# A buffer that nothing uses, ahead of the stage buffers of a two-layer trunk step

## The chip, the cores and the metric

The kernel runs on 1 core of a Trainium2 chip. The metric is device time in microseconds (us); the kernel before takes 2651.89 us, the median of 3 runs.

## What is computed

The reference is one inference step of a trunk with two layers (model width 2048), for 128 context tokens and 128 latent tokens. Layer 0 mixes tokens by differential attention beside grouped-query attention, layer 1 by a bidirectional mLSTM beside latent attention; each layer then has a gated FFN with a 3-tap convolution over tokens. Norms are RMS norms, and shift, scale and gate come from a conditioning vector through w_mod. Cut to what matters:

```python
for l in range(DEPTH):                               # DEPTH = 2
    mod = split(silu(cond) @ w_mod[l] + b_mod[l], 6)     # w_mod: 2048 x 12288
    h = rms(x, norm1_g[l]) * (1 + mod[1]) + mod[0]
    if l % 2 == 0:
        out = merge(diff_attention(...), gqa(...)) @ even_w_out   # from h @ even_w_in (2048 x 4608)
    else:
        out = merge(mlstm(...), mla(...)) @ odd_w_out             # from h @ odd_w_in (2048 x 4960)
    x = x + mod[2] * out
    h = rms(x, norm2_g[l]) * (1 + mod[4]) + mod[3]
    u = dwconv(h @ ffn_w_up[l], conv_w[l], conv_b[l])             # 2048 x 11264
    g, up = split(u, 2)
    x = x + mod[5] * ((silu(g) * up) @ ffn_w_down[l])             # 5632 x 2048
y = rms(x, final_norm_g)
```

The context tokens run as a second stream through the same weights, with a conditioning vector of their own. Everything is float32.

## The kernel before, in words

**Weights.** All large weights come as slabs of 512 KB (128 partitions x 2 chunks x 512 columns). `load_order` plans the order of all loads once, and SyncE issues them into 8 slots of `raw`. ScalarE rounds a slab to float32r in `w_hi` (`split_hi`, L491), VectorE subtracts to get the rest in `w_lo` (`split_lo`, L498); both hold 4 slabs. TensorE waits for `w_lo`, computes, and frees the slab.

**Products.** Tokens lie along the free dimension: both streams are 256 columns. An activation tile is split like a weight: in the stage's buffer `xs` (128 x 16 x 512, float32r) columns 0 to 255 of a chunk are the high part and 256 to 511 the low part. `three_products` (L633) computes one weight tile of 128 x 128 against 256 moving columns in three matmuls, each with a weight load of its own:

```python
pe.matmul(made, hi, x_hi, start=start and not second, ...)      # L636
pe.matmul(made, hi, x_lo, start=False, ...)                     # L637
return pe.matmul(made, lo, x_hi, start=False, stop=stop, ...)   # L638
```

In `pe.matmul(out, weights, moving)` the second operand is loaded into the array and the third streams past it. A slab is 2 chunks x 4 tiles x 3 products = 24 matmuls (`tile_products`, L640).

**Order.** Phases run one after another, and within a phase slabs in a fixed order (`Phase.seq`): modulation (`w_mod`), the even layer's input projection (72 slabs), its output projection, the FFN of layer 0 (up: 11 iterations x 2 groups x 8 slabs; down: 88 slabs), the odd layer's tail, q/k and v/o projections, latent query and key/value products, output projection, the FFN of layer 1. Modulation slabs (`mod_products`, L592) are spread over the phases up to the odd layer's v/o projection: after every 4 slabs of the phase come 4 modulation slabs, which break into the stream of the three products. The down projection of layer 0 and both parts of the FFN of layer 1 have none. Beside the products, ScalarE and VectorE do the splits, copies out of PSUM, convolution, attention and norms, placed by slab number.

**Places in SBUF.** A partition's buffers are laid out in the order in which `sb` (L319) is called. The persistent ones come first, in `trunk` at L326 to L343; the buffers of a stage are allocated inside a scope behind them and given back at its end, so that each stage starts at the same byte. In the built program of the kernel before the places per partition are, in bytes:

| buffer | starts at | past a multiple of 512 |
|---|---|---|
| raw, w_hi, w_lo, x (L326 to L329) | 16,512; 49,280; 65,664; 82,048 | 128 |
| m0, the last persistent one (L343) | 116,256 | 32 |
| first buffer of each stage: xs_even, acts, mix1 | 116,288 | 64 |
| xs_ffn of both layers (L1081) | 161,344 | 64 |
| xs_odd (L2210) | 179,264 | 64 |
| xs_out1b and xs_out1a, cq (L1905, L1906, L1900) | 182,336; 198,720; 182,336 | 64 |
| last end of any buffer (tb_out1) | 227,392 | |

A chunk of `xs` is 2048 bytes, its low part starts 1024 bytes behind its high part, and a full weight tile is 512 bytes wide. So all moving operands of the three products start 64 bytes past a multiple of 512, and all full weight tiles 128 past one. Two unused buffers are there already: `lead` (48 columns, L341) and `lead_odd` (24 columns, L2208), the second of which lies ahead of `xs_odd`. In the latent value products (`ukv_products`, L1957) the roles are changed: `w_hi` and `w_lo` move (256 columns in two pieces of 128), and the latent `ckv_hi` or `ckv_lo` is loaded.

Of the kernel before, what the change touches and what calls it, by code (L numbers as in the profile page):

```python
# [27 lines left out]
P = 128  # L28
# [287 lines left out]
def trunk(nc, ins, outs):  # L316
    ctx = ExitStack()
    with ctx:
        def sb(name, shape, dt=F32, scope=ctx):  # L319
            return scope.enter_context(nc.sbuf_tensor(name, shape, dt))  # L320
# [20 lines left out]
        lead = sb("lead", [P, LEAD_COLUMNS])  # L341
        gate_b = sb("gate_b", [4 * HEADS, 1])
        m0 = sb("m0", [2 * HEADS, 2])  # L343
        banks = ctx.enter_context(nc.psum_tensor("banks", [P, 8, 512], F32))

        ident = const[:, C_IDENT:C_IDENT + P]
# [2173 lines left out]
```

How the kernel before makes its waits and increments, by code:

```python
def wait(eng, sem, value):  # L177
    if not isinstance(value, int) or value > 0:
        eng.wait_ge(sem, value)
# [305 lines left out]
        def split_hi(act, f, i, o):  # L486
            q, s = f.own(i, o), f.own_at[o]
            act.wait_ge(*slab_landed(f, i, s))
            wait(act, slab_used.sem, q - SPLIT + 1)
            act.activation(w_hi[:, o % SPLIT], raw[:, s % RAW], ACT.Copy).then_inc(hi_done.sem, 1)
# [1 line left out]
        def split_lo(dve, f, i, o):  # L493
            q, s = f.own(i, o), f.own_at[o]
            dve.wait_ge(hi_done.sem, q + 1)
            wait(dve, slab_used.sem, q - SPLIT + 1)
            dve.tensor_tensor(w_lo[:, o % SPLIT], raw[:, s % RAW], w_hi[:, o % SPLIT].bitcast(F32),
                              ALU.subtract).then_inc(lo_done.sem, 1)
# [57 lines left out]
            def body(i, first, last):  # L557
                for s, (kind, g, k) in enumerate(f.seq):
                    if kind == "mod":
                        pe.wait_ge(*slab_landed(f, i, s))
                        mod_products(pe, f, i, s, g, k).then_inc(mod_used.sem, 1)
                    else:
                        o = f.own_at.index(s)
                        pe.wait_ge(lo_done.sem, f.own(i, o) + 1)
                        if k == 0:
                            out = 2 * (f.group(i, g) - 1)
# [28 lines left out]
        def copy_mod_rows(act, f, i, p):  # L596
            n = f.pair(i, p)
            act.wait_ge(mod_used.sem, f.mod_slab(i, MOD_SLABS * (PAIR * p + PAIR - 1) + MOD_SLABS - 1) + 1)
            wait(act, rows_turned.sem, n)
```

## Time and profile before

| what | us |
|---|---|
| median of 3 runs | 2651.89 |
| the 3 runs | 2647.7 to 2652.81 |
| the profiled execution's own time | 2675.88 |
| its span, from the first to the last instruction | 2674.1 |

The span is one profiled execution. PE is TensorE's matmuls, PEld its weight loads, DVE VectorE, ACT ScalarE, SP SyncE. A matmul's duration runs from its issue to its last result, and matmuls are pipelined: the step from one start to the next is much shorter than a duration. So the durations of a group add up to more than its share of the span, and the pace is read from counts in a stretch in which PE has no pause. A window's count holds every instruction of which a part lies in it.

### The profile page before, as it was taken

The page shows a single profiled execution, that of the slowest core. Times are in us where ns is not written, and L with a number is a line of the kernel's source. Part 1 is how long each engine was busy: PE and PEld are TensorE (multiplying, and loading weights), DVE is VectorE, ACT ScalarE, POOL GpSimd, SP SyncE. Part 2 cuts the span into 40 slices and gives each one's busy share as a digit, 9 for nine tenths or more (in the row PEclk, how much of TensorE's full clock was granted, in tenths as well). Part 3 has the DMA queues.
Part 4 walks back from the last instruction along what each step waited for, and adds up shares of the span by engine and source line. Part 5 has one row for each costly group of instructions (what it writes and reads, how often), then busy time and mean ns, then how long its engine had stood idle before and what let it go on. Part 6 is the DMA issues. An engine that isn't in the chain of part 4 may idle for free. (4 is left out here: it accounts for less than half of the span.)

```text
span 2674.1 us, 52531 instructions
## 1 busy us (share of the span) xinstructions
PE 2550.9 (95%) x20826; PEld 2328.3 (87%) x20826; DVE 1485.3 (56%) x1970; ACT 1295.8 (48%) x1795; POOL 11.7 (0%) x20
## 2 busy tenths in 40 slices
PE   6799999989999999999989999789899999999997
PEld 1487988878888888899989889778899999999997
DVE  1334455655454545577765445645655565567676
ACT  1443444364444444466565444334655555556553
POOL 0000000000000000000000000000000000000000
PEclk9999999989999999999989998889899999999999
DMA  9886665768888888865646884123455555555553
GB/s 388 330 317 233 231 228 184 289 256 309 318 316 319 314 318 313 321 212 192 203 128 234 321 299 142 62 93 114 156 189 186 184 187 185 185 188 187 176 186 107
DMA packets 170060, 608.28 MB, mean 227 GB/s; under 512 B 18688, under 2 KB 25152, under 8 KB 169648
## 3 DMA queue, kind: packets, MB, share of 16 engines
q1 hardware_dynamic: 168624, 600.33, 64.0%
q10 hardware_dynamic: 512, 2.97, 0.3%
q0 software_dynamic: 768, 2.79, 0.3%
q8 instruction: 112, 1.84, 0.3%
q14 instruction: 44, 0.36, 0.0%
HBM read 601.38 MB, written 4.63 MB: 227 GB/s over the span
## 5 line engine op out<-in xcount | busy, mean ns | idle before, releaser
L498 DVE TENSOR_TENSOR w_lo<-raw,w_hi 128x1024 fp32r<-128x1024 f32 x756 | 925.5, 1225 | 966.3 <-ACT w_hi L491 964.6
L491 ACT ACTIVATE w_hi<-raw 128x1024 fp32r<-128x1024 f32 x756 | 798.7, 1057 | 1018.2 <-PE banks L638 994.2
L636 PE MATMUL banks<-xs_ffn,w_hi 128*128 128x256 f32 x4224 | 1188.3, 281 | 5.2 <-DVE xs_ffn L792 5.0
L637 PE MATMUL banks<-xs_ffn,w_hi 128*128 128x256 f32 x4224 | 1181.9, 280 | 0.0
L638 PE MATMUL banks<-xs_ffn,w_lo 128*128 128x256 f32 x4224 | 1181.7, 280 | 0.0
L636 PEld LDWEIGHTS banks<-xs_ffn,w_hi 128*128 128x128 f32 x4224 | 797.8, 189 | 43.5 <-issue 42.6
L638 PEld LDWEIGHTS banks<-xs_ffn,w_lo 128*128 128x128 f32 x4224 | 803.8, 190 | 0.0
L637 PEld LDWEIGHTS banks<-xs_ffn,w_hi 128*128 128x128 f32 x4224 | 795.3, 188 | 0.0
L592 PE MATMUL banks<-raw,cond 128*32 128x512 f32 x1536 | 227.2, 609 | 29.2 <-DMA raw<-in_w_mod 18.0
L636 PE MATMUL banks<-xs_even,w_hi 128*128 128x256 f32 x832 | 241.8, 291 | 10.0 <-DVE w_lo L498 5.9
L637 PE MATMUL banks<-xs_even,w_hi 128*128 128x256 f32 x832 | 233.3, 280 | 0.0
L638 PE MATMUL banks<-xs_even,w_lo 128*128 128x256 f32 x832 | 233.2, 280 | 0.0
L636 PEld LDWEIGHTS banks<-xs_even,w_hi 128*128 128x128 f32 x832 | 158.8, 191 | 34.2 <-issue 22.9
L636 PE MATMUL banks<-xs_odd,w_hi 128*128 128x256 f32 (+2 forms) x640 | 181.3, 283 | 2.7 <-DVE xs_odd L792 2.6
L637 PE MATMUL banks<-xs_odd,w_hi 128*128 128x256 f32 (+2 forms) x640 | 179.0, 280 | 0.0
L638 PE MATMUL banks<-xs_odd,w_lo 128*128 128x256 f32 (+2 forms) x640 | 178.8, 279 | 0.0
L592 PEld LDWEIGHTS banks<-raw,cond 128*32 128x32 f32 x1536 | 43.5, 109 | 147.8 <-DMA raw<-in_w_mod 77.5
L637 PEld LDWEIGHTS banks<-xs_even,w_hi 128*128 128x128 f32 x832 | 158.4, 190 | 1.0 <-issue 1.0
L638 PEld LDWEIGHTS banks<-xs_even,w_lo 128*128 128x128 f32 x832 | 158.5, 190 | 0.0
L1071 DVE SCALAR_TENSOR_TENSOR y<-u,par,y 128x254 f32<-128x254 f32 x352 | 146.2, 478 | 20.5 <-ACT y L1058 17.6
L636 PEld LDWEIGHTS banks<-xs_odd,w_hi 128*128 128x128 f32 (+2 forms) x640 | 119.9, 187 | 14.0 <-issue 12.9
L1129 DVE TENSOR_TENSOR xs_ffn<-acts,xs_ffn 128x512 fp32r<-128x512 f32 x176 | 120.4, 684 | 0.0
(305 smaller groups left out, 2054.2 us busy)
## 6 DMA issues: line engine op xcount, KB each, us to landing
raw<-in_w_mod SPq DMA_DIRECT2D x384, 512.0 KB, 6.7
raw<-in_ffn_w_up SPq DMA_DIRECT2D x352, 512.0 KB, 3.5
raw<-in_ffn_w_down SPq DMA_DIRECT2D x176, 512.0 KB, 4.1
raw<-in_even_w_in SPq DMA_DIRECT2D x72, 512.0 KB, 4.0
raw<-in_odd_w_in SPq DMA_DIRECT2D x64, 512.0 KB, 4.5
raw<-in_even_w_out SPq DMA_DIRECT2D x32, 512.0 KB, 3.7
raw<-in_odd_w_out SPq DMA_DIRECT2D x32, 512.0 KB, 3.2
raw<-in_odd_w_tail SPq DMA_DIRECT2D x8, 448.0 KB, 3.7
```

Source lines behind the costliest of these rows:

```text
L491: act.activation(w_hi[:, o % SPLIT], raw[:, s % RAW], ACT.Copy).then_inc(hi_done.sem, 1)
L498: dve.tensor_tensor(w_lo[:, o % SPLIT], raw[:, s % RAW], w_hi[:, o % SPLIT].bitcast(F32), ALU.subtract).then_inc(lo_done.sem, 1)
L592: mm = pe.matmul(banks[quad:quad + QUAD, f.mod_bank(p), :], cond[:, n, columns], raw[:, s % RAW, c, :], start=n < QUADS and not second, st ...
L636: pe.matmul(made, hi, x_hi, start=start and not second, stop=False, skip_group_check=second)
L637: pe.matmul(made, hi, x_lo, start=False, stop=False, skip_group_check=second)
L638: return pe.matmul(made, lo, x_hi, start=False, stop=stop, skip_group_check=second)
L1071: added = dve.scalar_tensor_tensor(yt, ut, weight(f, i, g, which, t), yt, ALU.mult, ALU.add)
L1129: dve.tensor_tensor(xs[:, slot_of(s), NT:2 * NT], acts[:, chunk0(s):chunk0(s) + CHUNKS], xs[:, slot_of(s), 0:NT].bitcast(F32), ALU.subtrac ...
```

## The change

Behind `m0`, the last persistent buffer, a buffer of 112 columns of float32 is allocated, 448 bytes in each partition. Nothing reads or writes it. The whole diff:

```diff
@@ -341,6 +341,7 @@
         lead = sb("lead", [P, LEAD_COLUMNS])
         gate_b = sb("gate_b", [4 * HEADS, 1])
         m0 = sb("m0", [2 * HEADS, 2])
+        stage_pad = sb("stage_pad", [P, 112])
         banks = ctx.enter_context(nc.psum_tensor("banks", [P, 8, 512], F32))
```

So each stage's first buffer starts at 116,288 + 448 = 116,736 = 228 x 512, and all stage buffers that started 64 past a multiple of 512 start at one. The persistent buffers, `raw`, `w_hi`, `w_lo` and `x` among them, stay where they are.

## Rows read from the trace of the kernel before

**Rows 1.** The page: busy us, share of span, instructions; granted clock in tenths.

```profile
PE 2550.9 (95%) x20826; PEld 2328.3 (87%) x20826; DVE 1485.3 (56%) x1970; ACT 1295.8 (48%) x1795; POOL 11.7 (0%) x20
...
PEclk9999999989999999999989998889899999999999
```

**Rows 2.** Windows: length, busy (count) per engine, clock, DMA share, GB/s.

```profile
1160.00:1360.00 200.00, 200.00 (x1767) 200.00 (x1766) 144.77 (x170) 120.80 (x156) 0.00 (x0) 1.00 0.60 193
2000.00:2200.00 200.00, 200.00 (x1701) 200.00 (x1700) 119.12 (x148) 105.79 (x129) 0.00 (x0) 1.00 0.56 186
1920.00:2645.00 725.00, 724.82 (x6152) 724.30 (x6151) 460.48 (x559) 404.88 (x511) 0.00 (x0) 1.00 0.55 183
```

**Rows 3.** Groups by form, 1940 to 2640 us, PE: busy us, mean ns.

```profile
L636 PE MATMUL banks<-xs_ffn,w_hi 128*128 128x256 f32 x1982 | 556.9, 281 | 0.0
L638 PE MATMUL banks<-xs_ffn,w_lo 128*128 128x256 f32 x1982 | 556.9, 281 | 0.0
```

**Rows 4.** Groups by form, 1140 to 1370 us, PE.

```profile
L636 PE MATMUL banks<-xs_ffn,w_hi 128*128 128x256 f32 x676 | 186.7, 276 | 0.0
L637 PE MATMUL banks<-xs_ffn,w_hi 128*128 128x256 f32 x676 | 186.6, 276 | 0.0
L638 PE MATMUL banks<-xs_ffn,w_lo 128*128 128x256 f32 x675 | 186.3, 276 | 0.0
```

**Rows 5.** Groups by form, 1940 to 2640 us, weight loads.

```profile
L638 PEld LDWEIGHTS banks<-xs_ffn,w_lo 128*128 128x128 f32 x1982 | 380.5, 192 | 0.0
L636 PEld LDWEIGHTS banks<-xs_ffn,w_hi 128*128 128x128 f32 x1982 | 372.1, 188 | 0.0
```

**Rows 6.** Groups by form, 1140 to 1370 us, weight loads.

```profile
L638 PEld LDWEIGHTS banks<-xs_ffn,w_lo 128*128 128x128 f32 x676 | 126.9, 188 | 0.0
```

**Rows 7.** Windows between breaks of the first FFN's up projection.

```profile
620.00:630.00 10.00, 10.00 (x87) 10.00 (x86) 3.23 (x4) 3.45 (x4) 0.00 (x0) 1.00 0.86 317
634.00:643.00 9.00, 9.00 (x82) 9.00 (x82) 6.22 (x11) 4.79 (x6) 0.00 (x0) 1.00 0.86 294
646.00:656.00 10.00, 10.00 (x86) 10.00 (x87) 3.05 (x4) 3.18 (x3) 0.00 (x0) 1.00 0.90 334
```

**Rows 8.** Groups by form, 560 to 1140 us (first up projection), PE.

```profile
L637 PE MATMUL banks<-xs_ffn,w_hi 128*128 128x256 f32 x1395 | 388.7, 279 | 0.0
```

**Rows 9.** Groups by form, 1440 to 1620 us (odd layer's projections), PE.

```profile
L637 PE MATMUL banks<-xs_odd,w_hi 128*128 128x256 f32 x429 | 119.5, 278 | 0.0
```

**Rows 10.** The page's costliest groups, whole span: busy us, mean ns, idle before.

```profile
L498 DVE TENSOR_TENSOR w_lo<-raw,w_hi 128x1024 fp32r<-128x1024 f32 x756 | 925.5, 1225 | 966.3 <-ACT w_hi L491 964.6
...
L637 PE MATMUL banks<-xs_ffn,w_hi 128*128 128x256 f32 x4224 | 1181.9, 280 | 0.0
...
L637 PE MATMUL banks<-xs_even,w_hi 128*128 128x256 f32 x832 | 233.3, 280 | 0.0
...
L637 PE MATMUL banks<-xs_odd,w_hi 128*128 128x256 f32 (+2 forms) x640 | 179.0, 280 | 0.0
...
L1129 DVE TENSOR_TENSOR xs_ffn<-acts,xs_ffn 128x512 fp32r<-128x512 f32 x176 | 120.4, 684 | 0.0
```

**Rows 11.** DMA: the slabs' queue (packets, MB, share), and the stores of y.

```profile
q1 hardware_dynamic: 168624, 600.33, 64.0%
...
out_y<-y_out SPq DMA_DIRECT2D x4, 512.0 KB
```

**Rows 12.** A window in the latent value products, clock at half.

```profile
1754.60:1756.00 1.40, 1.40 (x8) 1.40 (x7) 0.01 (x1) 0.00 (x0) 0.00 (x0) 0.50 0.57 228
```

**Rows 13.** Timeline, the same products: start us, duration us.

```profile
1754.77 0.41 PE L1957 MATMUL banks<-w_hi,ckv_hi 128*128 128x256 f32 x1
...
1756.05 0.41 PE L1957 MATMUL banks<-w_hi,ckv_hi 128*128 128x256 f32 x1
```

**Rows 14.** Timeline, latent value products at full clock, first and last of 16.

```profile
1741.66 0.28 PE L1957 MATMUL banks<-w_hi,ckv_hi 128*128 128x256 f32 x1
...
1743.43 0.28 PE L1957 MATMUL banks<-w_hi,ckv_hi 128*128 128x256 f32 x1
```

## The prediction

> **What bounds the kernel now.** I read the page first. TensorE's matmuls cover 95% of the span, VectorE is busy for 56% and ScalarE for 48%, and the granted clock stands at 9 tenths or more in all but a few of the 40 slices [rows 1]. So the question is not who waits for whom but at what pace matmuls follow each other. For that I read windows: a count of matmuls in a stretch without a pause gives the step from one to the next. (A matmul that straddles an edge is counted, about 2.4 too many per window, 0.28 us each against a step of 0.115.) Two stretches of the same work, w_hi and w_lo against xs_ffn, both at clock 1.00 and with PE busy all through, differ: 1767 matmuls in 200 us in the first FFN's down projection, 1701 in 200 us in the second FFN [rows 2]. That is 200 / 1764.6 = 113.3 ns and 200 / 1698.6 = 117.7 ns: 4.4 ns apart, 3.9%.
>
> The groups by form say what differs. In the slow stretch each of the three products lasts 281 ns in the mean [rows 3], in the fast one 276 [rows 4]. In the slow stretch the weight load of one of the three, w_lo's, lasts 192 ns, the other loads 188 [rows 5]; in the fast stretch w_lo's too lasts 188 [rows 6]. Other traffic doesn't explain it: VectorE, ScalarE and DMA are all a little busier in the fast stretch than in the slow one [rows 2]. Nor does the place of the buffers alone: acts, xs_ffn and the weights lie at the same bytes in both FFNs. The pace is entered at a break of TensorE's stream and then kept. In the first FFN's up projection, where modulation products break in, three stretches in order hold 87, 82 and 86 matmuls in 10, 9 and 10 us [rows 7]: 118, 113 and 120 ns (one matmul more or less in a count is 1.2 ns), so slow, fast, slow. The form groups show the mix: the second product's mean is 279 ns over the whole of that up projection [rows 8] and 278 in the odd layer's input projections [rows 9], between 276 and 281.
>
> **The change, part by part.** It adds no instruction, wait, semaphore or transfer, and takes none away. Every buffer allocated behind it starts 448 bytes later. Moving operands go from 64 to 0 past a multiple of 512; split weights stay at 128. So the distance from moving operand to weights goes from 64 to 128 bytes.
>
> *VectorE and ScalarE on shifted buffers*: 0. A subtraction into xs_ffn (at 64 past) takes 684 ns for 512 columns, the split into w_lo (at 128 past) 1225 for 1024, 1.34 and 1.20 ns a column [rows 10], a difference that a fixed part per instruction accounts for. Should their durations change, the cover is wide: from 1920 to 2645 us VectorE works 460 of 725 us [rows 2], and would have to become 1.5 times as slow before TensorE waited.
>
> *Transfers into and out of shifted buffers*: 0. All the slabs, 600 of 608 MB, land in raw [rows 11], which isn't shifted; the few others lie beside TensorE's work, except the store of y at the end, 2 MB, of which I bound a change at 1 us either way.
>
> *The pace of the matmuls*: this is the whole sum, and before shows no other distance for these instructions. The bounds are the two paces. Counts first [rows 2, 10]: the second FFN's 6150 matmuls are all slow. In the first FFN's up projection and in the even and odd projections I take half as slow, by [rows 7 to 9]: half of 2 x 11 x 8 x 24 = 4224, of 3 x 832 = 2496 and of 3 x 640 = 1920, together 4320. Slow: 10,470. Fast: 3 x (4224 + 832 + 640) = 17,088 less these, 6618. (The 960 of the odd layer's output and latent query, up to 4 us, are left out.) If none were slow: 10,470 x 4.4 ns = 46 us less. If none were fast: 6618 x 4.4 ns = 29 us more.
>
> The profiled execution took 2675.88 us, 24.0 above the median of 2651.89. That is near the second FFN's share, 6150 x 4.4 = 27 us, so the unprofiled runs may already have that FFN at the fast pace; the trace cannot say. Then 46 - 27 = 19 us is left to gain. I take the ends 2652 - 46 = 2606 and 2652 - 19 = 2633, and the middle, **2620**: nothing puts it nearer to either.
>
> Why a gain rather than nothing: the loss exists only where two reads run at full rate. When the granted clock is at half, 1.2 GHz [rows 12], six steps of 256 columns take 1756.05 - 1754.77 = 1.28 us, 213.3 ns each [rows 13], which is 256 columns at 1.2 GHz with nothing lost. At 2.4 GHz the same columns would take 106.7, and take 113.3 or 117.7. So at full clock the operands don't arrive in time, the moving operand and the next weights are the two streams read in step, one of three weight loads is lengthened at the slow pace, and the change alters exactly the distance between these two.
>
> The Trainium skill, "SBUF — State Buffer", section "Who interferes with whom", speaks against the change: it gives TensorE two independent read ports, one for the moving operand and one for weight loads, and says TensorE never waits on anyone. By it the sum would be 0 and the time 2652, against 2620 by the rows. The lengthened loads [rows 5] do not fit it easily.
>
> **The rivals.** *No effect (2652).* The pace could be a matter of timing alone: where in the cycle a weight load is issued after a break. For it: the same bytes run at both paces, and no other engine's reads disturb either pace. Then the pad changes nothing, also not the moment of a break. That is also the case in which the change does not do what it is said to do. The rule of the Trainium skill cited above ("SBUF — State Buffer") gives this time. Chance 0.31, range 2647 to 2657.
>
> *Slower (2681).* The larger distance favours the slow pace. The place is the first matmuls after a break; it decides when the stretches now fast, the first FFN's down projection first (2112 matmuls, 9 us), are entered slow. For it: the only stretch where moving operand and weights lie otherwise, the latent value products, with w_hi moving at 128 and ckv stationary at 64, runs 15 steps in 1743.43 - 1741.66 = 1.77 us, 118 ns, slow [rows 14]. Against it: the moving operand there is cut in two pieces, and it is a short sample. Price 29 us, 2652 + 29 = 2681; with the second FFN now fast, 2708. Chance 0.30.
>
> *A deeper gain.* If the step from 106.7 to 113.3 is also one of placement, 17,088 x 6.6 ns = 113 us go as well: 2620 - 113 = 2507. For it is only the step at 1.2 GHz [rows 13]; against it, no stretch of these products shows such a pace. Chance 0.03. The Trainium skill, "TensorE: Matmul & The Clock Gate", section "Back-to-back issue gap", puts an isolated step at columns / 2.4 + 2.5 ns; by that, 109.2 here, an estimate, the time would be 2620 - 17,088 x 4.1 ns = 2550. No run here shows it.
>
> **How the numbers follow.** Forecast, the slow pace no longer entered: 0.36, its own range 2605 to 2636. With the deeper gain, faster by over 0.2% (5 us, about what a measurement can tell here) has 0.39; within 0.2%, 0.31; slower, 0.30. The signs are nearly even, because the trace shows that a second pace exists and what it costs, not what picks it. The 80% range runs from 2605 to 2690: it takes in the forecast, no effect, and the slower case's price with some 9 us to spare; left out are the deeper gain and the upper part of the slower case.
>
> **What would show it right or wrong.** Right: equal instruction counts, the window from 2000 to 2200 us holding 1765 matmuls rather than 1701, w_lo's loads at 188 ns, and products at 276 throughout. Wrong: the same 113 and 118 in the same stretches (no effect); 281 ns in the first FFN's down projection (slower); any stretch under 113 ns (deeper gain). If VectorE's or ScalarE's instructions on stage buffers change length, or a new wait stands ahead of the matmuls, my zeros were wrong.

## The result, and the profile after

| what | before | after |
|---|---|---|
| median of 5 runs, us | 2651.89 | 2721.49 |
| the runs, us | 2647.53 to 2652.81 | 2716.95 to 2723.61 |
| the profiled execution's own time, us | 2675.88 | 2720.27 |
| its span, us | 2674.1 | 2718.5 |

The ratio after / before is 1.0248, 95% interval 1.02 to 1.0295: slower by 69.6 us. The forecast was 2620, the range 2605 to 2690; the time lies above both. One line is new, so every line number behind L343 is one higher than before: the three products are now L637, L638 and L639.

The page of the kernel after: the span, busy time by engine, the granted clock in 40 slices, and the two VectorE groups that the prediction had costed at nothing.

```profile
span 2718.5 us, 52531 instructions
...
PE 2596.8 (96%) x20826; PEld 2377.0 (87%) x20826; DVE 1487.6 (55%) x1970; ACT 1295.9 (48%) x1795; POOL 11.8 (0%) x20
...
PEclk9999999989999999999999999799899999999999
...
L499 DVE TENSOR_TENSOR w_lo<-raw,w_hi 128x1024 fp32r<-128x1024 f32 x756 | 925.7, 1225 | 1008.7 <-ACT w_hi L492 1007.1
...
L1130 DVE TENSOR_TENSOR xs_ffn<-acts,xs_ffn 128x512 fp32r<-128x512 f32 x176 | 120.4, 684 | 0.0
```

Against [rows 1] and [rows 10]: the counts of instructions are the same on every engine, the clock is granted as before, the split into w_lo takes 1225 ns and the subtraction into xs_ffn 684 ns as before. It is TensorE's busy time that has grown: its matmuls' by 2596.8 - 2550.9 = 45.9 us, near the 2720.27 - 2675.88 = 44.4 us between the two profiled executions, against 2.3 us on VectorE. VectorE waits longer for ScalarE ahead of L499 (1008.7 us against 966.3), because the whole stream behind which both wait is slower.

The windows of the kernel after: length, busy time (count) of PE, PEld, DVE, ACT and POOL, the granted clock, the DMA share, GB/s. The first lies in the first FFN's down projection, the second in the second FFN.

```profile
1160.00:1360.00 200.00, 200.00 (x1688) 200.00 (x1687) 141.51 (x169) 116.42 (x150) 0.00 (x0) 1.00 0.57 191
2000.00:2200.00 200.00, 200.00 (x1688) 200.00 (x1687) 119.44 (x147) 104.58 (x127) 0.00 (x0) 1.00 0.54 184
```

Both stretches now hold 1688 matmuls, where [rows 2] show 1767 and 1701. With the same 2.4 straddlers taken off, a step is 200 / 1685.6 = **118.7 ns**. That is neither of the two paces of before (113.3 and 117.7): it is a third one, above both, and the same in both stretches, at a clock of 1.00 and with no pause. It is a mean: in the trace's second stretch single steps, from start to start, last 115 to 122 ns, where before they are 117 to 119.

The groups by form of the kernel after, 1940 to 2640 us, PE (busy us, mean ns):

```profile
L637 PE MATMUL banks<-xs_ffn,w_hi 128*128 128x256 f32 x1936 | 546.2, 282 | 2.5 <-DVE xs_ffn L793 2.4
L638 PE MATMUL banks<-xs_ffn,w_hi 128*128 128x256 f32 x1935 | 545.6, 282 | 0.0
L639 PE MATMUL banks<-xs_ffn,w_lo 128*128 128x256 f32 x1935 | 545.5, 282 | 0.0
```

The same view, 1140 to 1370 us:

```profile
L638 PE MATMUL banks<-xs_ffn,w_hi 128*128 128x256 f32 x635 | 178.7, 281 | 0.0
L639 PE MATMUL banks<-xs_ffn,w_lo 128*128 128x256 f32 x634 | 178.4, 281 | 0.0
```

The weight loads of the kernel after, 1940 to 2640 us:

```profile
L637 PEld LDWEIGHTS banks<-xs_ffn,w_hi 128*128 128x128 f32 x1936 | 365.6, 189 | 3.1 <-issue 2.9
L638 PEld LDWEIGHTS banks<-xs_ffn,w_hi 128*128 128x128 f32 x1936 | 365.6, 189 | 0.0
L639 PEld LDWEIGHTS banks<-xs_ffn,w_lo 128*128 128x128 f32 x1935 | 365.3, 189 | 0.0
```

A product lasts 281 to 282 ns everywhere, against 281 [rows 3] and 276 [rows 4]. But w_lo's loads are no longer the longer ones: 189 ns like the two others, against 192 [rows 5]. So this is not the 117.7 ns pattern of before with one lengthened load; all three steps of a tile pay about alike (118.7, 118.9 and 118.4 ns in the mean, by the starts in the second stretch).

Where the 69.6 us come from, by steps. The medians are best compared with a kernel before whose second FFN runs at 113.3 (the run `unchanged`, below, shows that the median execution does): 6336 matmuls of the second FFN x 5.4 ns = 34.2 us; 2112 of the first down projection x 5.4 = 11.4; the 8640 matmuls of the mixed stretches, at half 113.3 and half 117.7, from 115.5 to 118.7, 3.2 x 8640 = 27.6. Sum 73 us, measured 69.6. Between the two profiled executions the second FFN goes only from 117.7 to 118.7, 6.3 us: 6.3 + 11.4 + 27.6 = 45.3, measured 44.4.

### The profile page after: what moved, and what is told of

Its sections match the earlier page's. It is cut to its first block and busy times, and to the rows that moved or that the text cites. A ratio compares the mean times of both kernels' runs of the same rounds, so it can differ in the third digit from the quotient of the medians.

```text
span 2718.5 us, 52531 instructions
## 1 busy us (share of the span) xinstructions
PE 2596.8 (96%) x20826; PEld 2377.0 (87%) x20826; DVE 1487.6 (55%) x1970; ACT 1295.9 (48%) x1795; POOL 11.8 (0%) x20
## 5 line engine op out<-in xcount | busy, mean ns | idle before, releaser
L499 DVE TENSOR_TENSOR w_lo<-raw,w_hi 128x1024 fp32r<-128x1024 f32 x756 | 925.7, 1225 | 1008.7 <-ACT w_hi L492 1007.1
L637 PE MATMUL banks<-xs_ffn,w_hi 128*128 128x256 f32 x4224 | 1196.9, 283 | 4.9 <-DVE xs_ffn L793 4.8
L639 PE MATMUL banks<-xs_ffn,w_lo 128*128 128x256 f32 x4224 | 1192.0, 282 | 0.0
L638 PE MATMUL banks<-xs_ffn,w_hi 128*128 128x256 f32 x4224 | 1191.6, 282 | 0.0
L637 PEld LDWEIGHTS banks<-xs_ffn,w_hi 128*128 128x128 f32 x4224 | 798.1, 189 | 42.7 <-issue 41.7
L639 PEld LDWEIGHTS banks<-xs_ffn,w_lo 128*128 128x128 f32 x4224 | 797.7, 189 | 0.0
L638 PEld LDWEIGHTS banks<-xs_ffn,w_hi 128*128 128x128 f32 x4224 | 797.6, 189 | 0.0
L637 PE MATMUL banks<-xs_even,w_hi 128*128 128x256 f32 x832 | 244.8, 294 | 8.7 <-DVE w_lo L499 5.9
L638 PE MATMUL banks<-xs_even,w_hi 128*128 128x256 f32 x832 | 236.4, 284 | 0.0
L639 PE MATMUL banks<-xs_even,w_lo 128*128 128x256 f32 x832 | 236.4, 284 | 0.0
L637 PEld LDWEIGHTS banks<-xs_even,w_hi 128*128 128x128 f32 x832 | 159.0, 191 | 32.9 <-issue 22.5
L637 PE MATMUL banks<-xs_odd,w_hi 128*128 128x256 f32 (+2 forms) x640 | 182.9, 286 | 3.3 <-DVE xs_odd L793 3.2
L639 PE MATMUL banks<-xs_odd,w_lo 128*128 128x256 f32 (+2 forms) x640 | 180.8, 283 | 0.0
L638 PE MATMUL banks<-xs_odd,w_hi 128*128 128x256 f32 (+2 forms) x640 | 180.7, 282 | 0.0
L638 PEld LDWEIGHTS banks<-xs_even,w_hi 128*128 128x128 f32 x832 | 159.1, 191 | 1.0 <-issue 1.0
L639 PEld LDWEIGHTS banks<-xs_even,w_lo 128*128 128x128 f32 x832 | 158.8, 191 | 0.0
L637 PEld LDWEIGHTS banks<-xs_odd,w_hi 128*128 128x128 f32 (+2 forms) x640 | 119.1, 186 | 14.6 <-issue 13.5
```

What stands on the lines that cost most here:

```text
L499: dve.tensor_tensor(w_lo[:, o % SPLIT], raw[:, s % RAW], w_hi[:, o % SPLIT].bitcast(F32), ALU.subtract).then_inc(lo_done.sem, 1)
L637: pe.matmul(made, hi, x_hi, start=start and not second, stop=False, skip_group_check=second)
L638: pe.matmul(made, hi, x_lo, start=False, stop=False, skip_group_check=second)
L639: return pe.matmul(made, lo, x_hi, start=False, stop=stop, skip_group_check=second)
```

## The experiments

Two theories stood at the start, both compatible with the result. One (D in the texts): the pace is set by the **distance** from the moving operand's start to the weights' start, taken modulo 512 bytes; the change moved it from -64 to -128. The other (M): the **moving operand's own place** counts, and a start on a multiple of 512 is bad. A third: neither place counts, and the pace is a matter of timing. Every experiment only inserts unused buffers; nothing is computed otherwise. A column of a pad is 4 bytes. "Distance" is moving operand minus weights. Steps are worked out as above, 200 us / (count - 2.4).

### Distance or place

`unchanged`: the kernel before once more, no edit.

> The kernel before once more. 2652 us. If the profiled execution of before was 24 us longer because its second FFN ran at 117.7 ns, this one's second FFN should now show either pace, with a time of 2648 at 113.3 ns or 2676 at 117.7; if the profiler itself costs 24 us, it shows 117.7 ns at 2676 again or 113.3 at 2676.

Measured: 2651.83 us median of 8 runs, 2644.77 to 2682.89, ratio 1.0025 [0.9968, 1.0083]. Five of the 8 lie at 2645 to 2653, three at 2679 to 2683. The profiled execution took 2650.94. Its windows:

```profile
1160.00:1360.00 200.00, 200.00 (x1767) 200.00 (x1767) 144.94 (x170) 120.63 (x156) 0.00 (x0) 1.00 0.61 193
2000.00:2200.00 200.00, 200.00 (x1767) 200.00 (x1766) 122.49 (x151) 110.04 (x134) 0.00 (x0) 1.00 0.59 193
```

This time the second FFN runs at 113.3 ns, 1767 matmuls against the 1701 of [rows 2], and the execution is 2675.88 - 2650.94 = 24.9 us shorter. So the 24.0 us by which the profiled execution of before exceeded the median were the second FFN's pace, not a price of profiling. One and the same program has two times, by the pace at which that FFN is entered.

`both_shifted`: the pad goes ahead of all buffers, so weights and moving operands move together. Moving operands start at a multiple of 512 as in the change; the distance stays -64.

```diff
+        first_pad = sb("first_pad", [P, 112])
         raw = sb("raw", [P, RAW, CHUNKS, SLABW])
```

> 448 bytes ahead of raw: weights at 64 past a multiple of 512, moving operands at 0, so the distance of 64 bytes is that of the kernel before while the moving operands lie on multiples of 512 as in the changed kernel. Theory D (the distance from moving operand to weights sets the pace): about 2652 us, paces 113.3 and 117.7 ns. Theory M (the moving operands' own place, on a multiple of 512, sets it): about 2721 us, a mean step near 118.8 ns all through. Theory T (any shift draws the entry into a pace anew): anything from 2606 to 2708, with 113.3 and 117.7 the only paces.

Measured: 2662.15 us median of 10 runs, 2646.34 to 2676.95, ratio 1.0004 [0.9951, 1.0056]; half of the runs lie at 2646 to 2650, half at 2674 to 2677, the two times of the kernel before. Profiled 2649.68. Its windows:

```profile
1160.00:1360.00 200.00, 200.00 (x1768) 200.00 (x1767) 145.23 (x171) 120.31 (x156) 0.00 (x0) 1.00 0.61 193
2000.00:2200.00 200.00, 200.00 (x1767) 200.00 (x1766) 123.01 (x151) 109.46 (x134) 0.00 (x0) 1.00 0.59 194
```

`weights_moved`: the reverse. Moving operands stay at 64, the weights go to 192, so the distance is -128.

```diff
         raw = sb("raw", [P, RAW, CHUNKS, SLABW])
+        split_pad = sb("split_pad", [P, 16])
         w_hi = sb("w_hi", [P, SPLIT, CHUNKS, SLABW], F32R)
...
         m0 = sb("m0", [2 * HEADS, 2])
+        stage_pad = sb("stage_pad", [P, 112])
```

> 64 bytes between raw and w_hi, and 448 behind m0: weights at 192 past a multiple of 512, moving operands at 64 as before, distance 128 bytes as in the changed kernel. D: about 2721 us and the same mixture of steps from 115 to 122 ns, mean 118.8. M: about 2652 us and steps of 113.3 and 117.7. T: 2606 to 2708 with 113.3 and 117.7 alone.

Measured: 2720.71 us, 2718.12 to 2727.13, ratio 1.0246 [1.0168, 1.0324]. Its windows:

```profile
1160.00:1360.00 200.00, 200.00 (x1688) 200.00 (x1687) 141.51 (x170) 116.41 (x150) 0.00 (x0) 1.00 0.59 191
2000.00:2200.00 200.00, 200.00 (x1688) 200.00 (x1687) 119.46 (x147) 103.31 (x126) 0.00 (x0) 1.00 0.56 184
```

The same 1688 as the changed kernel, with moving operands where they were before. These two runs settle it: the place alone (`both_shifted`) costs nothing, the distance alone (`weights_moved`) costs the whole 69 us. M falls. The weights' own place can't be it either: the kernel before and the changed one have the same.

`row_further`: a pad of 512 bytes, one step further than the change; the distance is again -64 modulo 512.

```diff
         m0 = sb("m0", [2 * HEADS, 2])
+        stage_pad = sb("stage_pad", [P, 128])
```

> 512 bytes behind m0: every stage buffer lies 512 bytes further than in the kernel before, all places the same past a multiple of 512. If only the place past a multiple of 512 counts (D or M): 2652 us within 6, and the same paces in the same stretches. If a larger period counts, or any shift (T): another time, by up to 60 us.

Measured: 2674.35 us median of 10 runs, 2646.76 to 2680.31, ratio 1.0033 [0.9982, 1.0083]; four at 2647 to 2650, six at 2674 to 2680. Profiled 2648.77, with 1767 matmuls in both windows. A pad larger than the change's brings the kernel before back: that buffers move, and by how much, counts for nothing beyond the distance modulo 512. Timing alone, without place, is out as the cause of the slower time as well: the builds at -64 share their two times, and the two at -128 share the count of 1688.

### The pace by distance

The next pads lie where the change's lies and move only the distance, in steps of 64 bytes and then of 32.

`distance_0`:

```diff
         m0 = sb("m0", [2 * HEADS, 2])
+        stage_pad = sb("stage_pad", [P, 16])
```

> 64 bytes behind m0: moving operands at 128 past a multiple of 512, like the weights; distance 0. D1 (the pace worsens with the distance): no worse than the kernel before, 2606 to 2652 us, steps of 113.3 or less. D2 (what counts is whether the distance is an odd or an even multiple of 64): an even multiple, so 2721 us and a mean step of 118.8 ns.

Measured: 2739.81 us, 2736.02 to 2741.68, ratio 1.0343 [1.0323, 1.0363]. Its windows, and behind them in a fence of its own its first product by form, 1960 to 2640 us:

```profile
1160.00:1360.00 200.00, 200.00 (x1668) 199.70 (x1665) 139.33 (x170) 114.98 (x152) 0.00 (x0) 1.00 0.58 189
2000.00:2200.00 200.00, 200.00 (x1669) 200.00 (x1669) 116.63 (x142) 106.01 (x129) 0.00 (x0) 1.00 0.56 182
```

```profile
L637 PE MATMUL banks<-xs_ffn,w_hi 128*128 128x256 f32 x1879 | 533.1, 284 | 2.5 <-DVE xs_ffn L793 2.4
```

1669 matmuls are 120.0 ns, and a product lasts 284 ns. Duration and step move together: 276 - 113.3, 282 - 118.7 and 284 - 120.0 are all 163 to 164 ns. (The ends of matmuls are modelled in the profile, so the steps are what is measured.) D1 falls: the time rose where it should have stayed or fallen. D2 had the sign, but its 2721 us is 19 us short.

`distance_p64`:

```diff
         m0 = sb("m0", [2 * HEADS, 2])
+        stage_pad = sb("stage_pad", [P, 32])
```

> 128 bytes behind m0: moving operands at 192, 64 behind the weights. D1: as the kernel before, 2647 or 2676 us. D2: an odd multiple, so also 2647 or 2676 us with 113.3 and 117.7 ns; the latent value products, whose roles are changed, now have a distance of 64 the other way and keep 117.7.

Measured: 2702.65 us median of 5 runs, two at 2671 and 2673, three at 2703 to 2706, ratio 1.0161 [1.0082, 1.0241]. Profiled 2672.71, its windows:

```profile
1160.00:1360.00 200.00, 200.00 (x1701) 200.00 (x1699) 141.38 (x169) 115.93 (x150) 0.00 (x0) 1.00 0.59 188
2000.00:2200.00 200.00, 200.00 (x1767) 200.00 (x1766) 121.21 (x149) 111.27 (x135) 0.00 (x0) 1.00 0.59 192
```

The two paces of before, 117.7 and 113.3, but exchanged: now the down projection has the longer step. The two clusters of times, some 32 us apart, are near the price of the second FFN at the longer pace (6336 x 4.4 = 28 us); the profile shown is one of the lower cluster. D1 and D2 both missed the time: even the lower cluster is some 23 us above the 2648 of the kernel before. By the starts in the two traces, pauses left out, the stretches that mix both paces have mean steps of 117.5 (even projections), 117.8 (first up projection) and 116.4 ns (odd projections) here, against 115.3, 115.6 and 114.8 before. So +64 knows the same two paces as -64, but was at the longer one far more often: the sign of the distance counts too.

`distance_p128`:

```diff
         m0 = sb("m0", [2 * HEADS, 2])
+        stage_pad = sb("stage_pad", [P, 48])
```

> 192 bytes behind m0: moving operands at 256, 128 behind the weights. D1: about 2721 us as at 128 the other way. D2: an even multiple, about 2721 us.

Measured: 2719.59 us, 2717.4 to 2728.37, ratio 1.0277 [1.0249, 1.0306]; 1688 matmuls in both windows, 118.7 ns, as at -128.

`distance_p192`:

```diff
         m0 = sb("m0", [2 * HEADS, 2])
+        stage_pad = sb("stage_pad", [P, 64])
```

> 256 bytes behind m0: moving operands at 320, 192 behind the weights. D1: slower than 2721 us, or as slow. D2: an odd multiple, 2647 or 2676 us with steps of 113.3 and 117.7 ns.

Measured: 2653.72 us median of 9 runs, 2646.51 to 2678.28, ratio 0.9991 [0.9935, 1.0047]. Profiled 2677.99, its windows:

```profile
1160.00:1360.00 200.00, 200.00 (x1767) 200.00 (x1767) 145.42 (x171) 120.17 (x156) 0.00 (x0) 1.00 0.61 193
2000.00:2200.00 200.00, 200.00 (x1700) 200.00 (x1700) 118.26 (x146) 105.28 (x130) 0.00 (x0) 1.00 0.56 186
```

This is the pattern of [rows 2], at +192 instead of -64. So the sizes seen at -64 come back 256 bytes further; the next run asks that at 0.

`distance_256`:

```diff
         m0 = sb("m0", [2 * HEADS, 2])
+        stage_pad = sb("stage_pad", [P, 80])
```

> 320 bytes behind m0: moving operands at 384, 256 behind the weights. If the pace repeats every 256 bytes of distance: as at distance 0, 2740 us and steps of 120.0 ns. If it repeats only every 512: anything else, and at half a period the streams are farthest apart, 2606 to 2680 us.

Measured: 2737.99 us, 2736.3 to 2741.0, ratio 1.0262 [1.0167, 1.0357]; 1669 matmuls in both windows, 120.0 ns, the same as at distance 0 within one matmul. (The ratio is lower than at 0 because the kernel before stood at a median of 2677.14 beside it, more of its executions at the higher of its two times.) At the three pairs tried (0 and 256, -64 and 192, -128 and 128) the pace repeats after 256 bytes.

`distance_m32` and `distance_m96` ask what lies between the multiples of 64.

```diff
         m0 = sb("m0", [2 * HEADS, 2])
+        stage_pad = sb("stage_pad", [P, 8])
```

> 32 bytes behind m0: moving operands at 96, 32 ahead of the weights. If operands are read in lines of 64 bytes and only the line counts: moving operands stay in the line from 64 to 127, so 2648 or 2677 us and steps of 113.3 and 117.7 ns. If the distance counts byte by byte: between distance -64 and 0, steps of 116 to 119 ns and 2680 to 2720 us.

Measured: 2711.65 us, 2709.88 to 2713.21, ratio 1.016 [1.0066, 1.0253]. Its windows:

```profile
1160.00:1360.00 200.00, 200.00 (x1692) 200.00 (x1692) 142.18 (x169) 116.48 (x151) 0.00 (x0) 1.00 0.58 189
2000.00:2200.00 200.00, 200.00 (x1692) 200.00 (x1692) 119.15 (x147) 104.15 (x125) 0.00 (x0) 1.00 0.55 184
```

```diff
         m0 = sb("m0", [2 * HEADS, 2])
+        stage_pad = sb("stage_pad", [P, 120])
```

> 480 bytes behind m0: moving operands at 32 past a multiple of 512, 96 ahead of the weights. If only the line of 64 counts: as the changed kernel, 2721 us and a mean step of 118.7. If byte by byte: between distances -64 and -128, steps of 115 to 118 and 2660 to 2700 us.

Measured: 2710.22 us, 2704.57 to 2716.77, ratio 1.0165 [1.007, 1.026]. Its windows:

```profile
1160.00:1360.00 200.00, 200.00 (x1688) 200.00 (x1687) 140.87 (x168) 115.40 (x149) 0.00 (x0) 1.00 0.57 188
2000.00:2200.00 200.00, 200.00 (x1707) 200.00 (x1706) 118.98 (x146) 106.19 (x130) 0.00 (x0) 1.00 0.56 186
```

118.4 ns at -32, and 118.7 and 117.3 at -96: neither equals a neighbour at a multiple of 64 (120.0, 113.3 or 117.7, 118.7) throughout. That only the 64-byte line of a start counts falls with it. The reading byte by byte has the steps at -32, but at -96 both a step and the time lie above what it gave. All runs together, one distance for both weight buffers:

| distance modulo 256 | runs | steps, ns | median, us |
|---|---|---|---|
| 0 | distance_0, distance_256 | 120.0 | 2739.81, 2737.99 |
| -32 | distance_m32 | 118.4 | 2711.65 |
| -64 | before, unchanged, both_shifted, row_further, distance_p192 | 113.3 or 117.7 | 2651.83 to 2674.35 |
| -96 | distance_m96 | 118.7 and 117.3 | 2710.22 |
| 128 | after, weights_moved, distance_p128 | 118.7 | 2719.59 to 2721.49 |
| +64 | distance_p64 | 117.7 or 113.3 | 2702.65 |

The kernel before stood at the best of the distances tried.

### Different distances for w_hi and w_lo

`low_apart`: w_hi stays at -64, w_lo goes to -192, which is +64 modulo 256.

```diff
         w_hi = sb("w_hi", [P, SPLIT, CHUNKS, SLABW], F32R)
+        low_pad = sb("low_pad", [P, 32])
         w_lo = sb("w_lo", [P, SPLIT, CHUNKS, SLABW], F32R)
...
         m0 = sb("m0", [2 * HEADS, 2])
+        stage_pad = sb("stage_pad", [P, 96])
```

> 128 bytes between w_hi and w_lo and 384 behind m0: distance -64 to w_hi and -192 (+64) to w_lo, both of the two-paced kind. If each pair of moving operand and next weight load counts for itself: steps of 113.3 and 117.7 ns again, 2646 to 2690 us. If the pair of steps that shares one product's columns cannot lock at 117.7 when the loads differ: all at 113.3, about 2630 us. If the locks clash: up to 2720 us.

Measured: 2636.06 us, 2635.01 to 2639.87, ratio 0.9882 [0.979, 0.9974]. Its windows, and behind them the second product by form, 560 to 1140 us (first up projection):

```profile
1160.00:1360.00 200.00, 200.00 (x1767) 200.00 (x1766) 144.30 (x170) 119.72 (x154) 0.00 (x0) 1.00 0.59 190
2000.00:2200.00 200.00, 200.00 (x1767) 200.00 (x1766) 124.52 (x155) 109.76 (x133) 0.00 (x0) 1.00 0.57 193
```

```profile
L639 PE MATMUL banks<-xs_ffn,w_hi 128*128 128x256 f32 x1420 | 392.5, 276 | 0.0
```

113.3 ns in both windows, and 276 ns in the first up projection where [rows 8] have 279: the pace of 117.7 has gone from the mixed stretches too. This is the prediction's forecast, reached by another edit. A small rest is left: by the starts in the trace 13% of the tiles in the even projections, 4% in the first up projection and 4% in the odd projections still run at about 119 ns a step.

`low_apart_again`: the same kernel, in more runs.

> The best run once more, for its interval: 2636 us, all steps at 113.3 ns; against the kernel before 0.995 where that runs at 2648 and 0.985 where it runs at 2677.

Measured: 2639.51 us median of 12 runs, all of them between 2632.55 and 2644.6, against 2653.24 of the kernel before; ratio 0.9924 [0.989, 0.9957]. Its windows:

```profile
1160.00:1360.00 200.00, 200.00 (x1767) 200.00 (x1766) 144.52 (x171) 120.63 (x155) 0.00 (x0) 1.00 0.57 189
2000.00:2200.00 200.00, 200.00 (x1767) 200.00 (x1766) 125.02 (x155) 109.39 (x133) 0.00 (x0) 1.00 0.55 194
```

It is faster than both kernels, and the second time near 2677 did not come in 16 runs of the two.

`low_meets`: w_hi at -64, w_lo at 0.

```diff
         w_hi = sb("w_hi", [P, SPLIT, CHUNKS, SLABW], F32R)
+        low_pad = sb("low_pad", [P, 112])
         w_lo = sb("w_lo", [P, SPLIT, CHUNKS, SLABW], F32R)
...
         m0 = sb("m0", [2 * HEADS, 2])
+        stage_pad = sb("stage_pad", [P, 16])
```

> 448 bytes between w_hi and w_lo and 64 behind m0: moving operands at 64 past a multiple of 512, distance -64 to w_hi and 0 to w_lo. Each load counts for itself (one load in three is w_lo's): mean step (2 x 113.3 + 120) / 3 = 115.6 ns, about 2675 us. The worst distance sets all three: 120 ns, 2739 us. Any difference between the two loads is enough to keep 113.3: 2636 us.

Measured: 2738.41 us (2709.41, 2738.41, 2740.52), ratio 1.0277 [1.021, 1.0343]. Its windows:

```profile
1160.00:1360.00 200.00, 200.00 (x1701) 200.00 (x1700) 142.87 (x169) 117.25 (x152) 0.00 (x0) 1.00 0.58 194
2000.00:2200.00 200.00, 200.00 (x1638) 200.00 (x1637) 117.37 (x145) 100.32 (x121) 0.00 (x0) 1.00 0.51 179
```

1638 matmuls are 122.3 ns, more than at distance 0 for both; but the 1701 of the down projection are 117.7 ns, less than at distance 0 for both. A price per load that simply adds up falls: it gave 115.6 ns and 2675 us. So does the reading that one favourable distance is enough. That the worst pair sets the pace of all gave the time by luck: its 120.0 ns came in neither stretch. (Why one of the three runs took 2709 us stays open.)

In the second FFN one of the three products differs from the others, and that says something on which two reads meet. The three products by form, 1980 to 2640 us (in this kernel L638 is the first, L639 the second, L640 the third):

```profile
L639 PE MATMUL banks<-xs_ffn,w_hi 128*128 128x256 f32 x1801 | 522.3, 290 | 0.0
L640 PE MATMUL banks<-xs_ffn,w_lo 128*128 128x256 f32 x1801 | 508.9, 283 | 0.0
L638 PE MATMUL banks<-xs_ffn,w_hi 128*128 128x256 f32 x1800 | 508.6, 283 | 0.0
```

And two lines of its timeline: start us, duration us.

```profile
2100.03 0.29 PE L639 MATMUL banks<-xs_ffn,w_hi 128*128 128x256 f32 x1
2100.03 0.19 PEld L640 LDWEIGHTS banks<-xs_ffn,w_lo 128*128 128x128 f32 x1
```

The second product, which uses w_hi, is the one that became longer (290 ns against 283 of its neighbours), and w_lo's load starts together with it. The starts agree: from 2000 to 2200 us the mean step from the second product to the third is 127.5 ns, from the first to the second 121.7, from the third to the next tile 117.5. The matmul that pays most is the one during which w_lo is read, not the one that uses it. That suggests as the pair the moving operand being streamed and the next weights being loaded. It is not shown beyond this stretch. In the same kernel's down projection, at the same distances, the second product is no longer than the others (1140 to 1370 us: 281 ns, the others 281 and 282):

```profile
L639 PE MATMUL banks<-xs_ffn,w_hi 128*128 128x256 f32 x644 | 181.2, 281 | 0.0
```

`changed_low`: the moving operands of the change (w_hi at -128), w_lo at -64.

```diff
         w_hi = sb("w_hi", [P, SPLIT, CHUNKS, SLABW], F32R)
+        low_pad = sb("low_pad", [P, 112])
         w_lo = sb("w_lo", [P, SPLIT, CHUNKS, SLABW], F32R)
```

> 448 bytes between w_hi and w_lo, nothing behind m0: moving operands on multiples of 512 and distance -128 to w_hi as in the changed kernel, but -64 to w_lo. Each load for itself: (2 x 118.7 + 113.3) / 3 = 116.9 ns, about 2699 us. Worst distance sets all: 2721 us. Any difference is enough: 2636 us.

Measured: 2712.87 us (2707.31 to 2721.62), ratio 1.0218 [1.0163, 1.0273]. Its windows:

```profile
1160.00:1360.00 200.00, 200.00 (x1701) 200.00 (x1700) 142.01 (x169) 116.21 (x151) 0.00 (x0) 1.00 0.56 189
2000.00:2200.00 200.00, 200.00 (x1688) 200.00 (x1687) 117.89 (x143) 105.13 (x129) 0.00 (x0) 1.00 0.53 184
```

117.7 and 118.7 ns: giving w_lo alone its old distance back saves about 9 us of the change's 70, by 3 runs that spread over 14 us, where prices that add up gave 2699.

`swapped`: the two distances of `low_apart` exchanged, w_hi at +64 and w_lo at -64.

```diff
         w_hi = sb("w_hi", [P, SPLIT, CHUNKS, SLABW], F32R)
+        low_pad = sb("low_pad", [P, 32])
         w_lo = sb("w_lo", [P, SPLIT, CHUNKS, SLABW], F32R)
```

> 128 bytes between w_hi and w_lo, nothing behind m0: distance +64 to w_hi and -64 to w_lo, the two of the best run exchanged. If two different odd multiples of 64 keep the pace from locking at 117.7: all at 113.3, 2636 us. If w_hi needs -64: as at distance +64, 2671 or 2703 us.

Measured: 2669.38 us median of 10 runs, 2656.37 to 2704.41, ratio 1.0048 [1.0008, 1.0089]; seven runs lie at 2656 to 2672, three at 2695 to 2704. Its windows:

```profile
1160.00:1360.00 200.00, 200.00 (x1685) 200.00 (x1684) 138.79 (x163) 115.19 (x149) 0.00 (x0) 1.00 0.55 185
2000.00:2200.00 200.00, 200.00 (x1767) 200.00 (x1767) 121.97 (x150) 110.47 (x135) 0.00 (x0) 1.00 0.56 193
```

118.9 and 113.3 ns. So it is not enough that the two weight buffers differ by 128 bytes; it counts which of them has which distance. In the slow stretch it is again the second product that is longer, though w_lo is at -64 here (by form, 1140 to 1370 us):

```profile
L638 PE MATMUL banks<-xs_ffn,w_hi 128*128 128x256 f32 x639 | 180.8, 283 | 0.0
L637 PE MATMUL banks<-xs_ffn,w_hi 128*128 128x256 f32 x640 | 178.8, 279 | 0.0
```

The second product is also the only one that streams the low part of the activations. So what `low_meets` shows of it need not come from w_lo's distance of 0 alone.

## Why the prediction was wrong

**The step that failed** is "The bounds are the two paces." The prediction had seen that before shows no other distance, and still bounded the unknown distance by the two paces of the known one, 113.3 and 117.7 ns. They turned out to be the two paces of *one* distance. At 128 bytes there is one pace, 118.7 ns, outside the bounds, and it is not chosen at a break: 1688 matmuls in both windows, and by the starts 118.7 to 118.9 ns in the stretches that were mixed before. The forecast then took the better of the two bounds, and the range ended at 2690, 31.5 us under the result. The prediction reasoned that the change alters exactly the distance that matters, which the runs bear out (`both_shifted` and `weights_moved`), and read a gain from that; but that a distance matters says nothing of its sign, and the trace of before held no row on it.

**The slower rival** had the sign. Its price of 29 us was all matmuls at 117.7 ns against a profiled execution in which the second FFN already ran at that pace, and its 2708 allowed for that FFN at 113.3. The measured 2721.49 is 13 us above 2708: 17,088 matmuls x 1.0 ns, the third pace over the second, are 17 us. So its larger figure was short by the one term that nothing in the trace of before could give. Its mechanism, first matmuls after a break that decide, is not what happened: at this distance there is nothing to decide. The row that it leaned on, the latent value products at 118 ns with 128 against 64 [rows 14], pointed the right way, but that distance is +64, where `distance_p64` shows both paces.

**The no-effect rival** and the rule behind it fall. The Trainium skill, "SBUF — State Buffer", section "Who interferes with whom", gives TensorE two independent read ports, for moving operand and weight loads, and says that it never waits on anyone. The runs differ from what the prediction drew from that, a sum of 0: with equal instructions, equal clock and nearly equal traffic a step of the same matmul takes 113.3, 118.7 or 120.0 ns by the distance between moving operand and weights alone. The measurement decides.

**The deeper gain** did not show in any run: no window of these products held more than 1768 matmuls, 113.3 ns. The Trainium skill's figure for an isolated step ("TensorE: Matmul & The Clock Gate", section "Back-to-back issue gap"), an estimate of 109.2 ns here, was not reached in any run.

**What held.** The zeros: VectorE's and ScalarE's durations, the transfers (the last store of y took 5.03 us before and after) and the counts of instructions did not move, as the timeline's last line of the kernel after shows:

```profile
2710.79 5.03 SPq L2463 DMA_DIRECT2D out_y<-y_out  x4
```

The guess about the 24.0 us held: `unchanged` shows the second FFN at 113.3 ns in an execution at the median. The half shares of the mixed stretches were about right: with them the sum for the change is 73 us where 69.6 were measured. And the remaining gain of 19 us, 2633, if the longer pace is never entered, was near: `low_apart` has just that, at 2636.06 and 2639.51, a gain of 12 to 16 us on 2651.89. The share can be read from the starts: take a tile's three steps together and leave out tiles with a pause. In the trace of before 41% of the tiles in the even projections, 51% in the first up projection and 33% in the odd projections run at about 118 ns, in all 44% of the 8640 matmuls, 17 us; in `unchanged` it is 47%, 18 us. What `low_apart_again` still has at about 119 ns is 3 us, so 13 to 15 us were to be gained, and 2653.24 - 2639.51 = 13.7 were measured.

**Two small slips** change nothing above 1 us. The second FFN has 11 x 2 x 8 x 24 + 88 x 24 = 6336 matmuls; the 6150 of the sum are those of a window that leaves out a part of it. And one matmul more or less in a count of [rows 7] is 1.4 ns, not 1.2.

**What stays open.** What picks 113.3 or 117.7 ns after a break at a distance of 64; why 117.7 is not entered with w_hi at -64 and w_lo at +64, but the mirror image has 118.9 ns in one of two stretches; why the longer pace is so much more frequent at +64 than at -64; how the prices of two distances combine (122.3 ns in one stretch of `low_meets` is above that of its worse member, 117.7 in the other below it); and what lies between 113.3 ns and 106.7, half of the 213.3 that a step takes at half the clock [rows 13]. That the reads of moving operand and next weights collide in the memory is a reading that fits; the runs show the dependence on the distance, not the pair of reads for certain, nor the place where one waits.

## What to carry to other kernels

Where a stream of matmuls has no pause, read the step from the counts in a window, and try the distance between the moving operand's and the weights' buffers: here 64 bytes of it were worth 2.5%, without an instruction changed. With two weight buffers read in turn, try different distances for each; of four such pairs one, the pad of 32 columns ahead of the second and 96 behind the rest, gave 0.8%, its mirror image gained nothing, and the other two cost 2 to 3%. All this was measured for one shape, float32r weights of 128 x 128 against 256 columns with a load for each matmul; other shapes have to be tried. And when a change moves a quantity to a value that the trace never had, the values seen at the old one are no bounds: a range has to leave room on both sides of them.

## What the runs showed that was not expected

- The pace of these float32r matmuls (256 columns, full clock) depends on the distance modulo 256 bytes: 120.0 ns at 0, 118.4 at -32, 113.3 or 117.7 at -64 and +64, 118.7 at 128. 256 bytes further it repeats within one matmul: 1668 and 1669 matmuls at 0, 1669 at 256, 1688 at -128 and at +128.
- The kernel before has two times. Of 66 of its executions beside the experiments 41 took 2646 to 2656 us, 24 took 2673 to 2685, and one, not explained, 3784.64; the pace of one stretch of 6336 matmuls, 113.3 or 117.7 ns, accounts for the distance of 27 us (28 by the count). A median of few runs of such a kernel can lie at either.
- Where both weight buffers stand at a distance of 0, 64 or 128, windows of 200 us held 1668 or 1669, 1688, 1700 or 1701, or 1767 or 1768 matmuls and nothing between. So the mean step of a stretch without a break takes one of a few values.
